# A two-block transformer kernel: four modulation products move to the norms behind feed-forwards, and 32 convolution taps go to TensorE over shifted copies

## The reference, cut to what matters

```python
for i in range(DEPTH):            # second block
    m_lat = silu(c) @ ada_w[i] + ada_b[i]        # 9 * 1024 columns: shift, scale, gate, three times
    m_ctx = silu(c_ctx) @ ada_w[i] + ada_b[i]
    x   = x   + 0.5 * gt1 * swiglu(modulate(x, g1, sh1, sc1), wi, wo)   # and ctx alike
    y   = conformer_conv(modulate(x, g2, sh2, sc2), ...)    # layer 0; windowed attention in layer 1
    x   = x + gt2 * y
    x   = x + 0.5 * gt3 * swiglu(modulate(x, g3, sh3, sc3), wi2, wo2)

def conformer_conv(h, ...):
    u, g = split(h @ pw1_w + pw1_b, 2)
    u = u * sigmoid(g)
    u = depthwise_conv(u, dw_w, width=31, pad=15) + dw_b    # 31 taps a channel
    u = layer_norm(u);  return silu(u) @ pw2_w + pw2_b
```

## Time and profile before

| | us |
|---|---|
| median of 3 runs (lowest to highest) | 2899.5 (2895.69 to 2902.11) |
| the profiled execution | 2896.27 |
| its span | 2894.5 |
| PE busy | 2816.3 (97%) |
| DVE, ACT, POOL busy | 1634.3, 1268.1, 264.7 |
| convolution, from its first gate to the start of `pw2` | 1575 to 1756 |

### The profile page before, as it was taken

One profiled execution on the slowest core, in us unless ns is written; L12 is line 12 of the kernel. 1 busy time (PEld: TensorE's weight loads), 2 busy tenths in 40 slices (PEclk: granted clock), 3 DMA queues, 4 the chain that ended last, 5 costly groups with the idle time before them and its releaser, 6 DMA issues.

```text
span 2894.5 us, 46378 instructions
## 1 busy us (share of the span) xinstructions
PE 2816.3 (97%) x15926; PEld 2305.9 (80%) x15926; DVE 1634.3 (56%) x2891; ACT 1268.1 (44%) x2515; POOL 264.7 (9%) x249
## 2 busy tenths in 40 slices
PE   7999999999999999999999999999999999999998
PEld 7878788798787887788887546888887888877888
DVE  6766587567665876523335895423335233367765
ACT  4455554454555544523333435322334233246544
POOL 0001220000012200000001852000000000001000
PEclk9999999999999999999999999999999999999999
DMA  6666266555662666533332783423324233235453
GB/s 240 193 191 235 88 204 198 174 192 189 191 241 87 203 193 190 185 101 98 100 97 95 262 306 99 133 77 115 102 59 146 87 101 106 69 117 171 150 188 121
DMA packets 238867, 441.04 MB, mean 152 GB/s; under 512 B 26336, under 2 KB 28384, under 8 KB 238048
## 3 DMA queue, kind: packets, MB, share of 16 engines
q1 hardware_dynamic: 237568, 432.36, 46.5%
q0 software_dynamic: 1120, 6.29, 0.6%
HBM read 437.50 MB, written 1.05 MB: 152 GB/s over the span
## 4 chain that ended last, share of the span: by engine, by line
PE 88%; DVE 6%; POOL 2%; DMA 2%; ACT 1%; issue 1%; SPq 0%; POOLq 0%; DVEq 0%; ACTq 0%
PE ps L851 87%; DMA raw<-weights 2%; DVE low L2239 1%; DVE hidden L2242 1%; DVE zz L2242 1%; DVE x L2245 1%; POOL hidden L3030 1%; POOL hidden L2993 1%; ACT hidden L1673 1%; PE ps L1607 0%; DVE neg_max L2668 0%; PE ps L1399 0%; ACT high L1673 0%; DVE zz L2239 0%; DVE hidden L2239 0%
## 5 line engine op out<-in xcount | busy, mean ns | idle before, releaser
L851 PE MATMUL ps<-zz,high 128*128 128x512 f32 (+1 forms) x6720 | 1927.6, 365 | 1.6 <-DVE gated L2270 1.6
L851 PE MATMUL ps<-zz,low 128*128 128x256 f32 (+1 forms) x4160 | 1356.8, 330 | 44.2 <-DVE low L2239 30.4
L851 PEld LDWEIGHTS ps<-zz,high 128*128 128x128 f32 x6720 | 1205.5, 189 | 199.9 <-issue 2.6
L2239 DVE TENSOR_TENSOR low<-raw,high 128x512 fp32r<-128x512 f32 x1256 | 827.8, 700 | 410.9 <-ACT high L1673 408.5
L1673 ACT ACTIVATE high<-raw 128x512 fp32r<-128x512 f32 x1296 | 751.9, 623 | 512.5 <-PE ps L851 432.1
L851 PEld LDWEIGHTS ps<-zz,low 128*128 128x128 f32 x4160 | 787.2, 189 | 161.7 <-issue 37.3
L851 PE MATMUL ps<-high,zz 128*128 128x512 f32 (+2 forms) x1072 | 295.3, 360 | 2.1 <-DVE low L2239 2.1
L2239 DVE TENSOR_TENSOR hidden<-gated,ps 128x512 f32 (+1 forms) x74 | 48.6, 657 | 367.6 <-ACT gated L1673 367.6
L851 PEld LDWEIGHTS ps<-high,zz 128*128 128x128 f32 x1072 | 190.4, 189 | 36.8 <-issue 4.9
L2270 DVE TENSOR_REDUCE gated<-ps 128x512 f32<-128x1024 f32 x102 | 122.6, 1202 | 146.0 <-PE ps L851 146.0
L851 PE MATMUL ps<-low,zz 128*128 128x512 f32 (+3 forms) x544 | 196.1, 361 | 0.0
(11 more groups left out here) (206 smaller groups left out, 1732.6 us busy)
## 6 DMA issues: line engine op xcount, KB each, us to landing
raw<-weights SPq DMA_DIRECT2D x1634, 256.0 KB, 3.3
hidden<-norms POOLq DMA_DIRECT2D x4, 1024.0 KB, 5.9
cst<-consts SPq DMA_DIRECT2D x1, 1773.0 KB, 12.5
x<-x_in SPq DMA_DIRECT2D x1, 1024.0 KB, 5.8
x<-tokens_in POOLq DMA_DIRECT2D x1, 1024.0 KB, 12.3
x<-ctx_in POOLq DMA_DIRECT2D x1, 1024.0 KB, 6.2
out<-hidden SPq DMA_DIRECT2D x4, 256.0 KB, 2.4
```

The costliest lines, as they stand in the source:

```text
L851: return nc.tensor.matmul(out, lhsT, rhs, start=first, stop=last, **kw)
L2239: return nc.vector.tensor_tensor(out, a, b, op)
```

## The change

- `stream()` marks four groups as "aside": those come just ahead of the fill of each `post_norm` behind a first-block feed-forward (two layers, two feed-forwards). An aside group has no quarters in the ring. ACT issues one transfer of 2 MB in tile ASIDE_AT = 10 of the feed-forward, into the unused half of `hidden`, and `post_norm` on PE multiplies its eight parts (`aside_rows`) between turning the last rows and the usual fill, in a batch of two.
- The convolution has 14 fills instead of 18: 11 among the products (from the second half of tile 2 on, before from the second half of tile 1) and 3 in the tail (before 5). Batches are 4, 4, 6 instead of 4, 4, 4, 6.
- PE takes 12 taps of tile 6 and 20 of tile 7 (before 4 and 8), POOL and ACT 5 of tile 7 (before 9). So DVE has 8 taps less of each.
- Weights for these taps come from DRAM (`taps_in`, 512 KB, issued by ACT), and in place of spread diagonals there are four shifted copies of each 32 channels of `conv_in`, stacked on 128 partitions: SP issues 16 transfers from SBUF to SBUF for each of the two tiles, each 32 partitions by 550 or 558 floats (some 70 KB). One round of four strips does four taps. The copies of tile 6 are issued ahead of the load 1057 (the fourth quarter of the fill in the first half of tile 7), those of tile 7 ahead of the load 1083 (the sixth of the second tail fill). SP waits for `conv_taken` of the tile first.
- The terms of tile 6 come after the first tail fill, those of tile 7 after the last.

```diff
-SIDES = (0, 6, 8, 8, 8, 8, 8, 9)
+SIDES = (0, 6, 8, 8, 8, 8, 8, 5)
-CONV_FILLS = ((0, 0), (0, 1), (1, 1), (1, 1), (1, 1), (1, 1), (1, 1), (1, 1))
-TAIL_FILLS = 5
-PE_TERMS = {6: 4, 7: 8}
-CONV_BATCHES = (4, 4, 4, 6)
+CONV_FILLS = ((0, 0), (0, 0), (0, 1), (1, 1), (1, 1), (1, 1), (1, 1), (1, 1))
+TAIL_FILLS = 3
+ASIDE_AT = 10
+PE_TERMS = {6: 12, 7: 20}
+CONV_BATCHES = (4, 4, 6)
...
         yield from ffn(("ffn1", l))          # the same behind ffn2
+        yield aside()
         yield fills.pop()
...
+            def shifts(n):
+
+                w = rep_size(n)
+                sp.wait_ge(conv_taken, n + 1)
+                sp.wait_ge(quarter_done, used_by_gates[n] + RING)
+                for i in range(4):
+                    src, dst = conv_in[32 * i:32 * i + 32, n, 0, :], rep_of(n, i)
+                    for j in range(4):
+                        own = bass.AP(src.tensor, src.offset + SIDES[n] + j, [list(src.ap[0]), [1, w]])
+                        sp.dma_start(dst[32 * j:32 * j + 32, :], own).then_inc(shifts_landed[n], 16)
+
+            gates_end = max(DONE.values()) - 1
+            used_by_gates = {KT - 2: max(at for part, at in GATE_AT.items() if part[0] == KT - 2), KT - 1: gates_end + 1}
+            shift_at = {min(at for part, at in GATE_AT.items() if part[0] == KT - 1) + RING + 4: KT - 2, gates_end + RING + 3: KT - 1}
...
+                    if q in shift_at:
+                        shifts(shift_at[q])
                     slot_free(q)
                     load(q % RING, weights[q])
...
+            def aside_rows(self, rows):
+
+                if self.fills == 0:
+                    self.pe.wait_ge(cs_ready, 1)
+                self.pe.wait_ge(aside_landed, 16 * self.seen(aside_landed))
...
+                for k in range(KT):
+                    self.mm(ps[32 * (k % 4):32 * (k % 4) + 32, rows, :], cs[:, k, 10:42], aside(k), k < 4, False, skip_group_check=True)
+                self.in_batch = 1
...
-                self.fill(2, 3)
+                self.turn_rows(3)
+                if scale != ALPHA:
+                    self.aside_rows(2)
+                self.fill_rows(2)
...
+                def terms(n):
+
+                    pe.wait_ge(taps_landed, 16)
+                    pe.wait_ge(shifts_landed[n], 16 * 16)
+                    for m in range(PE_TERMS[n] // 4):
+                        for i in range(4):
+                            a = rep_of(n, i)
+                            moving = bass.AP(a.tensor, a.offset + 4 * m, [list(a.ap[0]), [S + 2 * PAD, 2], [1, S]])
+                            at = TERM_AT[n] + 128 * m + 32 * i
+                            o = self.mm(ps[32 * i:32 * i + 32, 2 * (n % 2) + 1, :], taps[:, at:at + 32], moving, m == 0, m == PE_TERMS[n] // 4 - 1,
+                                        skip_group_check=True)
+                    o.then_inc(terms_ready, 1)
 
                 for f in range(TAIL_FILLS):
-                    for half in range(2):
-                        if half == 0:
-                            self.turn_rows(7)
-                        self.fill_rows(6, range(4 * half, 4 * half + 4))
-                        for i in range(2 * (2 * f + half), min(2 * (2 * f + half) + 2, len(by_pe))):
-                            term(i)
+                    self.turn_rows(7)
+                    self.fill_rows(6)
+                    if f == 0:
+                        terms(KT - 2)
+                terms(KT - 1)
...
+                        if t == ASIDE_AT:
+                            nc.scalar.dma_start(hidden[:, 0:2 * KT, S:512], aside_in[self.asides]).then_inc(aside_landed, 16)
...
+                nc.scalar.dma_start(taps, taps_in).then_inc(taps_landed, 16)
                 half(0, 0)
...
-                    for i in range(len(by_pe) * (n - 1) // (KT - 2), len(by_pe) * n // (KT - 2) if n < KT - 1 else 0):
-                        m, t = by_pe[i]
-                        self.f(spread_w[i], c("ident"), ACT.Copy, scale=w[:, m, t:t + 1]).then_inc(weight_spread, 1)
...
-                        if (n, t) in ((0, 18), (1, TAPS - 6), (3, first + 8), (5, first + 8)):
+                        if (n, t) in ((1, first + 8), (3, first + 8), (5, first + 8)):
                             self.take_cols(7)
```

More of the change, by code:

```diff
@@ L244, in fill_batches @@
 def fill_batches():
[L245 to L250, removed]
+    before, beside = [], 0
+    for kind, *_ in stream():
+        if kind == "up_half":
+            break
+        if kind == "aside":
+            beside = 1
+        elif kind == "ada":
+            before.append(1 + beside)
+            beside = 0
+    conv, late = sum(CONV_BATCHES), LATE_FILLS + 1
+    return before + list(CONV_BATCHES) + [1] * (DEPTH * GROUPS - sum(before) - conv - late) + [late]
 def raw_quarters():
@@ L364, in lay_weights, with lay_aside, lay_taps @@
     return out
+def lay_aside(inp):
+    return np.stack([by_k(inp["ada_w_2"][l])[:, :, g * Q:g * Q + Q].reshape(P, 2 * KT, S) for kind, l, g, *_ in stream() if kind == "aside"])
+def lay_taps(inp):
+    w = inp["conv_dw_w_2"][0]
+    out = []
+    for n, terms in PE_TERMS.items():
+        own = w[SIDES[n]:SIDES[n] + terms, n * P:n * P + P].reshape(terms // 4, 4, 4, 32)
+        a = np.zeros((4, 32, terms // 4, 4, 32), np.float32)
+        for ch in range(32):
+            a[:, ch, :, :, ch] = own[..., ch].transpose(1, 0, 2)
+        out.append(a.reshape(P, terms * 32))
+    return np.concatenate(out, axis=1)
 def lay_norms(inp):
@@ L395, in now, with build @@
         return self.at.get(sem.name, 0)
-def build(nc, weights, consts, norms, x_in, tokens_in, ctx_in, out, n_quarters):
+def build(nc, weights, consts, taps_in, aside_in, norms, x_in, tokens_in, ctx_in, out, n_quarters):
     place, width = columns()
@@ L2373, in copy_cols @@
             def copy_cols(self, bank):
-                group = self.taken
-                assert BATCHES[self.took] == 1 and group < self.fills
+                first, n = self.taken, BATCHES[self.took]
                 self.took += 1
-                self.taken += 1
+                self.taken += n
+                assert self.taken <= GROUPS
                 self.dve.wait_ge(rows_turned, self.took)
-                nc.vector.tensor_copy(mods_raw[:].rearrange("p a k c -> p (a k c)")[:, 8 * (group % GROUPS):8 * (group % GROUPS) + 8],
-                                      ps[:, bank, 0:8].rearrange("p (i j c) -> p (j i c)", i=4, j=1)).then_inc(cols_taken, 1)
-                return group
+                nc.vector.tensor_copy(mods_raw[:].rearrange("p a k c -> p (a k c)")[:, 8 * first:8 * (first + n)].rearrange("p (j i c) -> p i j c", j=n, i=4),
+                                      ps[:, bank, 0:8 * n].rearrange("p (i j c) -> p i j c", i=4, j=n)).then_inc(cols_taken, 1)
+                return range(first, first + n)
             def modulations(self, groups):
@@ L2426, in post_norm @@
                 self.filled()
+                self.fills += scale != ALPHA
                 self.tokens_wait()
@@ L2457, in post_norm @@
                 if pending:
-                    group = self.copy_cols(3)
+                    groups = self.copy_cols(3)
                 for m in range(KT + 1):
@@ L2470, in post_norm @@
                             self.ahead(2 * k - 6)
-                        if k == 4 and pending and group % 2 == 1:
+                        if k == 4 and pending and any(g % 2 for g in groups):
                             v.wait_ge(cols_taken, self.took)
-                            self.modulation(group // GROUPS, group % GROUPS // 2)
+                            self.modulations(groups)
                         if k in (3, 5, 7):
@@ L3065 @@
     out = nc.dram_tensor("out", (P, KT, S), F32, kind="ExternalOutput").ap()
-    build(nc, aps["weights"], aps["consts"], aps["norms"], aps["x_in"], aps["tokens_in"], aps["ctx_in"], out, n_quarters)
+    build(nc, aps["weights"], aps["consts"], aps["taps_in"], aps["aside_in"], aps["norms"], aps["x_in"], aps["tokens_in"], aps["ctx_in"], out, n_quarters)
     res = run_bass_kernel_spmd(nc, [arrays], core_ids=[0])
```

41 lines of the change are left out of this document (29 added, 12 removed).

## The result

The changed kernel takes 2913.8 us (median of 5 runs, 2912.4 to 2915.5) against 2897.5 of the kernel before (5 runs, 2895.7 to 2902.1). The ratio is 1.0051, 95% interval 1.0040 to 1.0062: slower by 0.5%, where I forecast no change that can be measured (2901, range 2889 to 2911) and gave slower 0.25. The profiled span is 2910.6 us for 2894.5, 16.1 more. One of the nine executions of `late2` (experiment 7) took 3956 us at a granted clock of 0.65 for the others' 0.99, and is left out of its interval.

What follows compares the result with a forecast made beforehand. PE's sequence bounds the kernel, in the convolution a five-engine loop, then the tail's loads. Convolution -4.1, norm ahead -0.5, four norms +6.9 sum to +2.3 us on the median 2899.5: 2901.8, said as 2901, range 2889 to 2911.

Steps and rivals of the forecast that it cites:

- the price of a copy: Convolution: each of SP's copies taken at 0.42 us an issue, 6.7 us for 16; bounds nothing and 11.0 us.
- Rival C: Copies dear: at 0.69 us an issue each set costs 4.3 us more on PE's path; +10.9, 2910.4; chance 0.11.
- Front: Convolution's product groups: two fills leave the front, so gate 2 and on to gate 6 come 6.7 us earlier.
- First set: Tile 7's first half: copies ahead of load 1057 make PE's second group 8.5 us late; last product ends at 1705.5.
- Tail: After the last product: 11.4 us fewer loads, against a second copy set and terms; first mean 4.1 us earlier overall.
- Terms: End of the tail: 2.9 us for tile 6 lie under the loads, 4.8 for tile 7 come last and count.
- Norm ahead of the convolution: Norm before the convolution: turning rows moves behind the fill, where ACT's root waited 0.54 us for PE; -0.5 us.
- Four norms: Norms behind first-block feed-forwards: moved products add 1.3 us in the first and 1.86 in each of three others, +6.9.
- F: Four norms: moved products run beside something, so the +6.9 is partly missing; counted with hidden copies, together 0.25.
- 2 MB transfers: Feed-forwards: the 2 MB transfers issued by ACT are hidden; without that cover 5.7 us each.
- E: Feed-forwards: the 2 MB transfers starve the ring, up to 5.7 us each, +25, 2925; chance 0.06.
- Copies one after another: Both sets: each copy begins when the last has landed, 30.1 us more per set, twice, 2961; chance 0.02.

Runs made afterwards that it cites:

- `late2`: Kernel before with only the products moved (old taps), put behind the norms' transposes, ACT's row copy at the second tile; 2890.6 us, ratio 0.9971.
- experiment 7: Kernel with moved products and old taps, products put behind the transposes: 2900.5 us; with ACT's row copy at the second tile (`late2`): 2890.6 us.
- experiment 3: Changed kernel with each copy cut into two of half the width: 2932.7 us; with all copies read from the tile's first column: 2913.6 us.
- experiment 6: Changed kernel with 38 filling matmuls where PE waits for load 1057 in tile 7's first half: 2912.6 us, ratio 1.0046.
- Experiment 9: Second profiles, unchanged: kernel before 2900.0 us; only taps over copies 2922.6; `late2` 2891.8; `late2` with taps over copies issued by ACT 2890.4.
- `bounce`: Changed kernel with each copy set made as one write to HBM and four reads of 128 rows: 2923.0 us, ratio 1.0075.

## Why the prediction was wrong

**The step that failed** is the price of a copy: "I take 0.42, between the first two, since a copy is smaller than a load but comes in a burst". It measured 0.633 with its gap (0.590 and 0.04), near the upper bound of 0.69 from the one row of another form. As a pace 0.42 was even below that of the loads, 0.47 with the gap, which is 0.8 us of a set. The reason that I gave, size, is what experiment 3 refutes: a copy of half the size costs the same. A set is 3.4 us longer than in my sum, and both sets lay on PE's path as I had said, so 6.8 us come from this term. Rival C said just this, "decides from 0.53", and by it the time is 2908 to 2909 at 0.63; I gave it 0.11.

**What the sum left out** is what PE's wait does to its clock: 3.0 us behind the first gap (experiment 6). The trace of before had one such stretch (clock 0.98 over 1000 to 1200 us, 6.8 us of it at half clock behind idle time of PE), and I did not carry it over to a gap that I forecast myself. In the tail the half clock (1735.0 to 1741.9) costs nothing that shows: PE waits for a load before each quarter there, and takes one every 0.67 us, as at the full clock behind it (0.69).

Point by point:
- *Front*: right, -6.6 us to gate 6 for -6.7.
- *First set*: place and kind of the wait right. Last product group at 1719.96 - 8.8 = 1711.2 in the old clock, forecast 1705.5. Of the 5.7 us, 3.4 are issues and 3.0 the clock, less 0.7 elsewhere.
- *Tail*: 30.5 us from the last product group to the first mean, forecast 25.6, before 30.5. Of the 4.9 us 3.4 are issues and 1.5 SP's arrival at the set, 4.1 us behind the last product group instead of 2.6. Removed quarters and copies cancel to nothing, where I had a gain of 4.1 in all.
- *Terms*: 4.7 us for tile 7 on the path (1745.71 to 1750.44), forecast 4.8. DVE waits 9.98 us for them, as said.
- *Norm ahead of the convolution*: -0.5, right.
- *Four norms*: +1.1 and 3 x 1.7 = 6.3 for 6.9, right, and no part hidden (F): experiment 7 shows that they could be.
- *2 MB transfers*: hidden; the feed-forwards show no step, so E is out.
- *Copies one after another* (D): out. They go out every 0.63 us and land in 2.0 to 4.7.
- *Steps near 300 us and ahead of block 2*, 3.2 us of the profiled span: not in the sum. Experiment 9 shows that such a step can come without the change and comes more often with it, so some of these 3 us belong to the change. How many, no run isolates.

The Trainium skill's fixed time of about 2.0 us for a transfer (DMA: Bandwidth & Descriptors, Anatomy of one DMA) is fitted there to transfers that GpSimd issues, which the prediction didn't say. The landings of these copies, issued by SP, agree with it: 2.0 to 2.1 us for 70 KB when nothing else moves, 2.2 by the fit. It concerned a term that didn't matter; what mattered is how long the issuing queue is held.

## What to carry to other kernels

Price a small transfer by its issue and not by its bytes, take the row of the dearest form until one of the same form is there, and put it in the queue of an engine that waits anyway, not in the one whose loads the bound engine waits for. Before moving a step past a wait, list who counts what stands behind it: two of my experiments moved the wait to a counter and a row copy that I hadn't listed. Where you forecast a gap on PE, add the slower clock behind it, and take more than one profile before a step of 2 to 4 us is put down to an edit; the mean granted clock of every execution says how often it comes.

## What the runs showed of the hardware

- A DMA from 32 partitions of SBUF to 32 partitions holds SP for 0.590 us, with rows of 1.1 or 2.2 KB alike, and ACT for 0.61 (median of 32, of 2.2 KB); a 256 KB load of 128 rows from HBM holds SP for 0.43.
- Such copies, one every 0.63 us, land in 2.0 us on idle DMA engines and, issued by ACT, in up to 6.9 among the loads.
- Reads from HBM of 128 rows of 2.2 KB, with four shifts as the outer dimension of the source, moved 93 GB/s at a DMA share of 0.25 while they were alone (`bounce`, 1709.8 to 1713.4 us); loads of 128 rows make 366 at 1.01.
- After a wait of 11.8 us PE stood at 1.2 GHz until 5.9 us after it took up work (1705.3 to 1711.2); 38 filling matmuls of 512 columns in the wait kept it at 2.4 GHz (`filler`).
- With the same program, a stretch of attention ran at 2.4 GHz in one execution and at 1.2 GHz for 13.7 us in another, 4.0 us of time. Over 58 executions of that program on one chip the mean granted clock went from 0.992 to 0.999.
